# Seven products instead of eight in the last quarter of an MLP's second product

## The reference

```python
h = rmsnorm_2(x, g_norm2[l]) * (1.0 + sc2) + sh2
x = x + gt2 * (jnp.square(jax.nn.relu(h @ w1[l])) @ w2[l])
```

## Time and profile before

| what | value |
|---|---|
| median of 3 runs | 975.77 us (975.66 to 976.11) |
| the profiled execution, its own time | 975.91 us |
| its span | 974.1 us |
| TensorE busy | 958.2 us, 98% |
| VectorE busy | 676.3 us, 69% |
| ScalarE busy | 548.7 us, 56% |
| GpSimd busy | 83.4 us, 9% |
| moved by DMA | 148.70 MB |

### The profile page before, as it was taken

How to read it: one execution, slowest core, us unless ns; L and a number is a source line. 1 busy time by engine, 2 the same in 40 slices (tenths; PEclk the granted TensorE clock), 3 DMA queues, 4 the chain that set the end, 5 groups by cost and what they waited for, 6 DMA issues and landing times.

```text
span 974.1 us, 13132 instructions
## 1 busy us (share of the span) xinstructions
PE 958.2 (98%) x4712; PEld 799.3 (82%) x4712; DVE 676.3 (69%) x1237; ACT 548.7 (56%) x1085; POOL 83.4 (9%) x173
## 2 busy tenths in 40 slices
PE   8999999999999999999999999999999999999998
PEld 7878998978888888777787887798888888888886
DVE  6487888878788767668678886756535853774773
ACT  6448787753223257479887564655735644734520
POOL 4000000011121112000010000110000001000000
PEclk9999999999999999999999999999999999999999
DMA  8205222139787644734444224355867577573201
GB/s 298 84 24 185 68 67 98 58 140 352 279 318 281 177 146 149 268 108 121 115 150 123 73 66 156 147 124 136 210 204 182 161 216 185 118 222 125 86 33 55
DMA packets 36674, 148.70 MB, mean 153 GB/s; under 512 B 9193, under 2 KB 9193, under 8 KB 24706
## 3 DMA queue, kind: packets, MB, share of 16 engines
q1 hardware_dynamic: 23970, 101.41, 30.5%
q0 software_dynamic: 9568, 42.48, 16.6%
q10 hardware_dynamic: 3072, 3.98, 1.2%
HBM read 138.32 MB, written 5.27 MB: 147 GB/s over the span
## 4 chain that ended last, share of the span: by engine, by line
PE 84%; DVE 7%; ACT 5%; issue 2%; DMA 1%; POOL 0%; ACTq 0%; DVEq 0%; POOLq 0%
PE psum L2109 25%; PE psum L2110 24%; PE psum L2111 24%; PE psum L2277 3%; PE psum L2256 2%; PE psum L2306 2%; PE psum L2309 1%; DVE wl L1264 1%; DMA raw<-in_wall 1%; ACT two L1009 1%; DVE hl L1304 1%; ACT wh L702 1%; PE psum L2540 1%; DVE xt L1300 1%; ACT p_sb L836 0%
## 5 line engine op out<-in xcount | busy, mean ns | idle before, releaser
L2109 PE MATMUL psum<-hh,wh 128*128 128x512 f32 (+1 forms) x720 | 273.9, 380 | 0.7 <-DVE hl L1304 0.6
L2111 PE MATMUL psum<-hh,wl 128*128 128x512 f32 (+1 forms) x720 | 267.4, 371 | 0.0
L2110 PE MATMUL psum<-hl,wh 128*128 128x512 f32 (+1 forms) x720 | 267.2, 371 | 0.0
L1264 DVE TENSOR_TENSOR wl<-raw,wh 128x512 fp32r<-128x512 f32 x328 | 214.1, 685 | 45.6 <-ACT wh L702 45.1
L702 ACT ACTIVATE wh<-raw 128x512 fp32r<-128x512 f32 x328 | 189.0, 621 | 80.7 <-PE psum L2111 63.7
L2109 PEld LDWEIGHTS psum<-hh,wh 128*128 128x128 f32 x720 | 135.3, 188 | 24.5 <-DVE hl L1304 1.8
L2111 PEld LDWEIGHTS psum<-hh,wl 128*128 128x128 f32 x720 | 135.2, 188 | 23.8
L2110 PEld LDWEIGHTS psum<-hl,wh 128*128 128x128 f32 x720 | 135.5, 188 | 20.9 <-issue 1.0
L2109 PE MATMUL psum<-wh,ah 128*128 128x512 f32 x224 | 88.5, 395 | 0.0
L2111 PE MATMUL psum<-wh,al 128*128 128x512 f32 x224 | 87.3, 390 | 0.0
L2110 PE MATMUL psum<-wl,ah 128*128 128x512 f32 x224 | 87.2, 389 | 0.0
(11 more groups left out here) (336 smaller groups left out, 1632.8 us busy)
## 6 DMA issues: line engine op xcount, KB each, us to landing
raw<-in_wall SPq DMA_DIRECT2D x78, 1024.0 KB, 5.3
raw<-in_wall POOLq DMA_DIRECT2D x15, 1024.0 KB, 7.9
wa<-in_wada POOLq DMA_DIRECT2D x24, 512.0 KB, 6.0
gt<-in_wada POOLq DMA_DIRECT2D x20, 512.0 KB, 6.8
xt<-in_xcols SPq DMA_DIRECT2D x8, 264.0 KB, 8.3
cb<-c_rows SPq DMA_DIRECT2D x8, 264.0 KB, 3.5
x<-in_x SPq DMA_DIRECT2D x4, 512.0 KB, 10.2
x_kept<-x SPq DMA_DIRECT2D x4, 512.0 KB, 2.9
```

Source lines behind the costliest of these rows:

```text
L1264: e.tensor_tensor(home(w)[1][:, cs], raw_of(w, c), home(w)[0][:, cs].bitcast(F32), ALU.subtract).then_inc(v["wl"], 1)
L2109: e.matmul(out_, lh, rh, start=start, stop=False, skip_group_check=True)
L2110: e.matmul(out_, lh, rl, start=False, stop=False, skip_group_check=True)
L2111: return e.matmul(out_, ll, rh, start=False, stop=stop, skip_group_check=True)
```

## The change

The second stage of quarter 3 takes seven products too, in the order 1, 2, 6, 5, 7, 4, 3 (`LAST_ORDER`, loop variable r = 0 to 6), with the halves made in its first stage as in the other quarters (with other signs). Four of the products, 1, 6, 7 and 4, are added up one after the other in the same two banks, 4 and 5: ScalarE copies the banks after product 1 (p1), after 6 (u2) and after 7 (u3) (`last_copy`), and after product 4 they hold the part of c21. Products 5 and 3 are added up in banks 6 and 7 in the same way; VectorE reads them after product 5 (p22). The gated blocks c12, c21, c11 and c22 of the quarters before, and p11 and p22 of this one, are no longer added to the residual by VectorE: GpSimd issues a DMA with `accum_op` for each block of 128 x 512, SBUF to SBUF, two to a pair, and each pair waits until the pair before has landed (`to_residual`, semaphore `res`). ScalarE's stores stand at its program's end and wait for these. SP loads one unit more, and GpSimd issues in quarter 3 five DMAs that add up weights. Two semaphores of the kernel's start are also merged into one.

```diff
-PRODUCTS = (1, 2, 7, 6, 5, 3, 4)
+ORDER = (1, 2, 7, 6, 5, 3, 4)
+LAST_ORDER = (1, 2, 6, 5, 7, 4, 3)
 P_BANK = {1: (2, 3), 2: (0, 1), 7: (2, 3), 6: (0, 1), 5: (2, 3), 3: (4, 5), 4: (6, 7)}
+LAST_BANK = {1: (4, 5), 2: (2, 3), 6: (4, 5), 5: (6, 7), 7: (4, 5), 4: (4, 5), 3: (6, 7)}
...
-X3 += [(3, name, b) for name in ("u2", "u3", "c12a", "c22", "c11", "c12", "c21") for b in range(2)]
-X3 += [(3, op, ch, i) for ch in range(2) for i in range(4) for op in ("*c", "+c")]
-X3 += [(3, op, ch, i) for ch in range(2) for i in range(4) for op in ("*", "+")]
+X3 += [(3, name, b) for name in ("u2", "u3", "c12a", "c12", "c22", "c21", "c11", "*c12", "*c21", "*c11", "*c22",
+                                 "p11", "*11", "*u", "-u", "p22", "*22", "*21", "+21") for b in range(2)]
+X3 += [(3, op, b) for b in range(2) for op in ("*12", "+12")]
...
+        block_at = {"c11": sums[1], "c12": sums[6], "c21": sums[7], "c22": sums[5]}
+        p1_last = sums[2]
+        u2_last, u3_last = (s_f[0][:, 0:512], s_f[1][:, 0:512]), (s_f[2][:, 0:512], s_f[3][:, 0:512])
...
-            place.update(zip(range(o_, o_ + 11), (a2, a3, a0, a1, a2, a3, a1, a0, a2, a3, a1) if q_ < 3 else places[q_]))
+            place.update(zip(range(o_, o_ + 11), (a2, a3, a0, a1, a2, a3, a1, a0, a2, a3, a1) if q_ < 3 else
+                             (a2, a3, a0, a2, a1, a0, a3)))
...
+                e.wait_ge(v["wl"], 4 * (o + 5) + 4)
+                load(u + 4 + 1, a3)
...
+            def last_copy(r, b):
+                e.wait_ge(t["w2"], 42 + 2 * r + b + 1)
+                if r == 0:
+                    e.wait_ge(v["x3"], N_X3[3, "c11", b])
+                else:
+                    e.wait_ge(v["sl"], 48)
+                e.activation({0: p1_last, 2: u2_last, 4: u3_last}[r][b], bank[4 + b], ACT.Copy).then_inc(a["acc"], 1)
...
+                    if q == 3 and r % 2:
+                        for b in range(2):
+                            last_copy(r - 1, b)
...
+            e.wait_ge(d["res"], 160)
+            store(0, 0)
+            store(1, 0)
+            e.wait_ge(d["res"], 192)
+            store(2, 1)
+            store(3, 1)
+            for b in range(2):
+                e.wait_ge(v["x3"], N_X3[3, "+21", b])
+                store(2 + b, 0)
+            for b in range(2):
+                e.wait_ge(v["x3"], N_X3[3, "+12", b])
+                store(b, 1)
...
+            def gated(name, b):
+                c, ch = block_at[name][b], int(name[2]) - 1
+                if (name, b) == ("c12", 0):
                     e.wait_ge(d["gt"], 32)
+                e.wait_ge(v["x3"], N_X3[3, name, b])
                 e.tensor_tensor(c, c, gt[:, 1, 512 * ch:512 * ch + 512], ALU.mult).then_inc(v["x3"], 1)
+            def last_11(op, b):
+                c = p1_last[b]
+                if op == "p11":
+                    e.wait_ge(t["w2"], 42 + 2 + b + 1)
+                    e.wait_ge(a["acc"], 10 + b + 1)
+                    e.tensor_tensor(c, c, bank[2 + b], ALU.add).then_inc(v["x3"], 1)
+                else:
+                    e.wait_ge(v["x3"], N_X3[3, "p11", b])
+                    e.tensor_tensor(c, c, gt[:, 1, 0:512], ALU.mult).then_inc(v["x3"], 1)
+            def last_u(op, b):
+                c, o = u2_last[b], x2[:, b, 512:1024]
+                if op == "*u":
+                    e.wait_ge(a["acc"], 12 + b + 1)
+                    e.tensor_tensor(c, c, gt[:, 1, 512:1024], ALU.mult).then_inc(v["x3"], 1)
+                else:
+                    e.wait_ge(v["x3"], N_X3[3, "*u", b])
+                    e.wait_ge(d["res"], 32)
+                    e.tensor_tensor(o, o, c, ALU.subtract).then_inc(v["x3"], 1)
+            def last_22(op, b):
+                c = u3_last[b]
+                if op == "p22":
+                    e.wait_ge(t["w2"], 42 + 6 + b + 1)
+                    e.wait_ge(a["acc"], 14 + b + 1)
+                    e.tensor_tensor(c, bank[6 + b], c, ALU.subtract).then_inc(v["x3"], 1)
+                else:
+                    e.wait_ge(v["x3"], N_X3[3, "p22", b])
+                    e.tensor_tensor(c, c, gt[:, 1, 512:1024], ALU.mult).then_inc(v["x3"], 1)
+            def last_21(op, b):
+                c, o = tmp[:, b, :], x2[:, 2 + b, 0:512]
+                if op == "*21":
+                    e.wait_ge(t["w2"], 42 + 10 + b + 1)
+                    e.tensor_tensor(c, bank[4 + b], gt[:, 1, 0:512], ALU.mult).then_inc(v["x3"], 1)
+                else:
+                    e.wait_ge(v["x3"], N_X3[3, "*21", b])
+                    e.wait_ge(d["res"], 64)
+                    e.tensor_tensor(o, o, c, ALU.add).then_inc(v["x3"], 1)
+            def last_12(b):
+                c, o = u2_last[b], x2[:, b, 512:1024]
+                e.wait_ge(t["w2"], 42 + 12 + b + 1)
+                e.wait_ge(v["x3"], N_X3[3, "-u", b])
+                e.tensor_tensor(c, bank[6 + b], gt[:, 1, 512:1024], ALU.mult).then_inc(v["x3"], 1)
+                e.wait_ge(v["x3"], N_X3[3, "*12", b])
                 e.tensor_tensor(o, o, c, ALU.add).then_inc(v["x3"], 1)
+            def last_step(f, *ops):
+                for op in ops:
+                    for b in range(2):
+                        f(op, b)
...
                     elif q == 3 and j == 2:
+                        last_step(gated, "c12")
...
+                    if q == 3 and r == 5:
+                        last_step(last_22, "p22")
+                    if w + 1 < NW:
+                        for c in range(4):
+                            lower(w + 1, c)
+                    if q == 3 and r == 0:
+                        last_step(gated, "c21")
+                    elif q == 3 and r == 1:
+                        last_step(gated, "c11", "c22")
+                    elif q == 3 and r == 2:
+                        last_step(last_11, "p11")
+                    elif q == 3 and r == 3:
+                        last_step(last_11, "*11")
+                    elif q == 3 and r == 4:
+                        last_step(last_u, "*u", "-u")
+                    elif q == 3 and r == 5:
+                        last_step(last_22, "*22")
+            last_step(last_21, "*21", "+21")
+            for b in range(2):
+                last_12(b)
...
+            TO_RESIDUAL = ("*c12", "*c21", "*c11", "*c22", "*11", "*22")
+            def to_residual(name):
+                n = TO_RESIDUAL.index(name)
+                if n:
+                    e.wait_ge(d["res"], 32 * n)
+                src = {"*11": p1_last, "*22": u3_last}[name] if n > 3 else block_at[name[1:]]
+                for b in range(2):
+                    i, ch = 2 * (int(name[-2]) - 1) + b, int(name[-1]) - 1
+                    e.wait_ge(v["x3"], N_X3[3, name, b])
+                    e.dma_start(x2[:, i, 512 * ch:512 * ch + 512], src[b], accum_op=ALU.add).then_inc(d["res"], 16)
+            for q in range(4):
                 o, (a0, a1, a2, a3) = W_MLP + 11 * q + 4, places[q]
-                e.wait_ge(d[f"w{a0}"], 16 * n_load[o + 2])
-                add(q, 2, a0)
-                e.wait_ge(d[f"w{a1}"], 16 * n_load[o + 3])
-                add(q, 2, a1)
-                e.wait_ge(d[f"wa{a1}"], 192 + 16 * n_add[o + 3] - 16)
-                add(q, 0, a1)
+                o3, o2 = o + order(q).index(7), o + order(q).index(6)
+                if q < 3:
+                    e.wait_ge(d[f"w{place[o3]}"], 16 * n_load[o3])
+                    add(q, 2, place[o3])
+                e.wait_ge(d[f"w{place[o2]}"], 16 * n_load[o2])
+                add(q, 2, place[o2])
+                e.wait_ge(d[f"wa{place[o2]}"], 192 + 16 * n_add[o2] - 16)
+                add(q, 0, place[o2])
+                if q == 3:
+                    e.wait_ge(d[f"w{place[o3]}"], 16 * n_load[o3])
+                    add(q, 2, place[o3])
+                    to_residual("*c12")
                 e.wait_ge(v["wl"], 4 * o + 4)
                 add(q, 2, a2)
-                e.wait_ge(v["wl"], 4 * (o + 3) + 4)
-                add(q, 3, a1)
+                if q == 3:
+                    to_residual("*c21")
+                    to_residual("*c11")
+                e.wait_ge(v["wl"], 4 * o2 + 4)
+                add(q, 3, place[o2])
                 if q == 0:
                     gate(1)
+            to_residual("*c22")
+            to_residual("*11")
+            to_residual("*22")
...
+            def last_product(r):
+                p, w = LAST_ORDER[r], W_MLP + 37 + r
+                upper, lower = home(w)
+                for b in range(2):
+                    if p == 1:
+                        e.wait_ge(v["x3"], N_X3[3, "c12", b])
+                    elif p == 2:
+                        e.wait_ge(a["r"], 30)
+                    elif p == 5:
+                        e.wait_ge(v["x3"], N_X3[3, "c21", b])
+                    elif p == 3:
+                        e.wait_ge(v["x3"], N_X3[3, "p22", b])
+                    else:
+                        e.wait_ge(a["acc"], 10 + {6: 0, 7: 2, 4: 4}[p] + b + 1)
+                    for k in range(4):
```

(8 more changed lines are left out.)

150 lines of the change are left out of this document (47 added, 103 removed).

## The result

The changed kernel takes 979.73 us (median of 5, 979.52 to 979.98), the one before 975.98 (975.66 to 976.11). The ratio is 1.0041, interval 1.0028 to 1.0054. The profiled execution took 979.73 us, and its span is 977.9.

The account below looks back on a forecast made before the run. TensorE, busy 98% of the span, bounds the kernel. Span 974.1 minus 5.4 (24 matmuls) plus 3.0 (store burst) gives 971.7, a gain of 2.4 to 2.6; forecast time 973.3 us, range 970.3 to 977.0.

Parts of the forecast that it names:

- the 5.44 us for 24 matmuls: TensorE, last MLP quarter: seven block products for eight save 24 matmuls at 0.2267 us, 5.44 us.
- the stages and their times up to 953.8: Quarter 3: last hidden block ends at 926.63, then products back to back every 5.44 us, the fifth ending at 953.83.
- that the copies and conversions fit while the weights are in time: ScalarE and VectorE in the seven products: each slack over 1 us, so costed at zero.
- the rate of an adding DMA: GpSimd's adding DMAs: 1 MB holds the engines 5.69 us; by bytes, 256 KB is 1.42 us.
- the end 6 us behind the landing of *22: Kernel's end: six 256 KB stores bunched behind *22's landing at 965.6, span ending at 971.6.
- that each pair's price counts five times: GpSimd's chain: past 6 us, each further us per pair counts about five times (c21, c11, c22, *11, *22).
- the slower one, the DMA chain as the bound: Rival, chance 0.13: pairs past 6 us set the end; at 6.4 time passes 977.7, at 8 about 984.
- I take 5.2: GpSimd's residual DMAs: a pair of 256 KB adds takes 5.2 us, between estimates of 4.9 and 5.4.
- Seen at 950.5: Weight add for r = 5, behind *c11: issued about 941.3, seen at 950.5, 2.1 us late for ScalarE, without stalling TensorE.
- some 4 us: In the slower rival at 8 us a pair, weights seen at 957 stall TensorE some 4 us before product r = 5.
- ScalarE's copies of u3: ScalarE before the last products: u3 copied from 953.83, with no delay to TensorE expected.
- 22 at 965.6: Last residual pair: *22 ready at 960.4, landing at 965.6 after a 5.2 us pair.

Follow-up runs that it names:

- the version with VectorE's additions: The changed kernel's seven products, but all additions to the residual on VectorE and no residual DMA; 971.69 us, ratio 0.9961 to the kernel before.
- the first experiment: The changed kernel with the weight add for r = 5 issued ahead of the pairs of c21 and c11; 982.92 us, ratio 1.0075 to the kernel before.
- 979.68: The 970.74 kernel with the pairs of c21 and c11, chained, put back ahead of the weight add for r = 5; 979.68 us, ratio 1.0041.
- 970.74: Seven products with VectorE's additions, but c21 and c11 by unchained adding DMAs behind the weight add; 970.74 us, ratio 0.9951 to the kernel before.
- 974.91: The 971.69 kernel (all additions on VectorE), but p11 and p22 by two chained adding pairs at the end; 974.91 us, ratio 0.9992.

## Why the prediction was wrong

**Right:** the 5.44 us for 24 matmuls; the stages and their times up to 953.8 (within 0.5 us); that the copies and conversions fit while the weights are in time (no wait of TensorE in the version with VectorE's additions); the rate of an adding DMA; the end 6 us behind the landing of *22 (5.9); that each pair's price counts five times; and the place where it would hurt, the weight add behind the pairs of c21 and c11. The rival that came true is the slower one, the DMA chain as the bound, which I priced at 977.7 from 6.4 us a pair and gave 0.13.

**The step that failed** is the price of a pair, "I take 5.2". For a pair issued together it was right: 5.3 (c22 in the first experiment). But GpSimd doesn't always issue both together. I had bounded the transfer's length, and left out a bound on the issue. In the changed kernel it was 6.5, 7.3, 10.5 (c22, with the weight add in it) and 7.2 us from the first issue of a pair to that of the next, and 5.2 from the issue of *22 to its landing. Three had their second half held until all before had landed; c21 ran beside SP's load issued at 934.01, in two of the later runs with 9.7 and 9.8 us for the pair; that the load is the cause wasn't tested. The trace of before couldn't show it, as GpSimd there never had two DMAs at once in this part of the program, except one that nobody waited for (the gate rows behind an add, 697.07). That was a hint: it landed after 10.2 us where the same copy elsewhere took 4.1, and I didn't use it.

**What followed.** "Seen at 950.5" became 955.67. I had found the slack before TensorE stalls to be about 2 us beyond it, and 5 us were more. The wait of 4.1 us looks like the "some 4 us" that I had for slow pairs, but that agreement is luck. Mine was for weights seen at 957 and a TensorE that waits for `wl`. It waited for ScalarE's copies of u3, which I had at 953.83 and free, and which in ScalarE's program stand behind the late unit's conversion. The first lower part was ready at 957.0, so 2.7 us of the wait are the weights and 1.4 the copies. That the granted clock would fall behind the wait, and cost 2.9 us more, I had left out of every case. Neither delayed the end, as *22 didn't depend on them. Then *22 at 965.6 became 971.95, 6.4 us later, and the stores carried that to the end unchanged: 971.6 + 6.3 = 977.9.

**Two chains, not one.** The chain of waits in the profile runs through the late weights. It isn't the whole cause: with them in time the kernel was 3.2 us slower, since the pairs had moved behind, and that chain alone then cost 11.2 us over the version without residual DMAs (982.92 against 971.69). Each chain was also cut out by itself: the late weights cost 9.0 us (979.68 against 970.74), the last two pairs 3.2 (974.91 against 971.69). In the changed kernel the two run beside each other, so their costs don't add up. The 9.0 is more than the late weights cost there: in that run they came later, 29.7 us behind the start of the last hidden block's upper part where the changed kernel has 27.3, and four additions of VectorE's stand behind them. An estimate for the changed kernel is its last addition at 973.54 with the old tail of 2.5, a span of 976.0 where the stores behind *22 made it 977.9. The range failed for the same reason: I gave slow pairs too little weight, with nothing in the trace that excluded them.

**Still open:** what decides which issue is held. It was the fifth, eighth and tenth DMA from the add for r = 3 in the changed kernel, others in other versions, rarer with more room. The rule of the room wasn't found.

## What to carry to other kernels

An engine's DMA queue is a program in order: before putting work that nobody waits for ahead of a transfer that somebody does, look at who waits behind it. A chain of transfers, each behind the landing of the one before, has to be priced per link and multiplied, with the issue as well as the data; where a link isn't in the trace, the factor belongs in the range. And when a stall is removed and nothing is won, a second chain ended just as late: cut each out alone, from the good side.
